# A hybrid decoder layer on one core: tokens loaded in transposed layout, with the RMS-norm row factor applied behind the projections

## The chip, the cores and the metric

The kernel runs on one NeuronCore of a Trainium2 chip. Its time is device time in microseconds, the median of several runs; lower is better.

## What is computed

One decoder layer for 2048 tokens of width 1024, in fp32:

```python
h = rms_norm(x, attn_norm_g)        # x * rsqrt(mean(x*x) + eps) * g
z = h @ w_in                        # q, k, v of attention; q, k, v, gate of retention; pooling input
ya = sliding_window_attention(...)  # 6 query heads, 2 kv heads, window 128, sinks, relative bias
yr = retention(...)                 # 6 heads, chunks of 128, rotary on q and k, recurrent state
yp = pool_mixer(...)                # trailing means over 2, 4, 8, 16 positions
x = x + concat(ya, yr, yp) @ w_out
x = x + square(relu(rms_norm(x, mlp_norm_g) @ w_up)) @ w_down
return rms_norm(x, final_norm_g)
```

The factor rsqrt(mean(x*x) + eps) belongs to a token, the gain g to a channel. In a product h @ w_in the gain has to be in before the sum over channels; the token's factor can be applied to the result.

## The kernel before

The work has two parts. The **mixer** goes through the tokens in four quarters of 512 (`QT`), three in a hardware loop and the last written out with the first steps of the second part mixed in. The **feed-forward part** then goes through all tokens in two passes.

Every large product is made of three matmuls: each operand is split into a high part, rounded to the faster fp32r format on ScalarE (a copy), and a low part, the rest, on VectorE (a subtraction). TensorE sums high x low, low x high and high x high (`three`, lines 2016 to 2018).

A quarter of the mixer runs through 39 output tiles of one PSUM bank each, in three banks in turn (`dense`): tiles 0 to 5 and 22 are projections with channels in partitions (`proj_T`: three of q, then k, v, and twice the pooling input), tiles 6 to 21 are the retention projections with tokens in partitions (`proj_G`), tiles 23 to 38 the output projection (`out_tile`). Between them stand the small products of attention, retention and pooling. Weights come in 27 units of 512 KB a quarter (`NU`), through three staging buffers (`stage`) into a ring of six split pairs: `split_hi` on ScalarE (line 887), `split_lo` on VectorE (line 1550). SyncE (SP) issues the loads in the order of `mixer_loads`; unit u is issued once unit u-3 is split.

The tokens of a quarter are loaded twice. One copy, `xn`, is squared on ScalarE for the row sums (`square_x`, line 906); POOL makes the factor `rstd` (lines 756 and 758); VectorE multiplies by factor and gain (`x_norm`, line 1351); TensorE transposes the result, 8 blocks of 128x128 for each of the four token blocks (`norm_transposes`, line 2045); ScalarE and VectorE split it into `hT_hi` and `hT_lo` (lines 927 and 1358). For the next quarter this is done ahead, between the last output tiles. Tile 0 is made in two halves of 256 tokens (`proj_first`). The other copy, `xq`, is the residual: VectorE adds the output tiles to it (`evac_x2`, line 1507), ScalarE issues its store to DRAM (line 911) and squares it for the second norm (line 919).

At the very start TensorE makes the rows of the relative-position bias (line 2008, fp32, 33 partitions). They go to DRAM and come back shifted.

All engines run fixed orders of instructions and meet at semaphores. A wait holds everything that is behind it on its engine, the DMA issues of SP too.

## Time and profile before

| | us |
|---|---|
| median of 3 runs | 2063.99 |
| lowest, highest | 2061.77, 2064.23 |
| the profiled execution | 2064.74 |
| its span in the trace | 2062.9 |
| TensorE busy | 2036.2 |
| VectorE busy | 1382.3 |
| ScalarE busy | 922.5 |
| POOL busy | 185.9 |

The trace is of one execution. Times in it count from the start of the span. PE is TensorE, DVE VectorE, ACT ScalarE, POOL GpSimd, SP the engine that issues most DMAs. A matmul row shows 0.39 us for 512 columns, but such matmuls overlap; what one costs is the distance between the starts of two.

### The profile page before, as it was taken

The page shows a single profiled execution, that of the slowest core. Times are in us where ns is not written, and L with a number is a line of the kernel's source. Part 1 is how long each engine was busy: PE and PEld are TensorE (multiplying, and loading weights), DVE is VectorE, ACT ScalarE, POOL GpSimd, SP SyncE. Part 2 cuts the span into 40 slices and gives each one's busy share as a digit, 9 for nine tenths or more (in the row PEclk, how much of TensorE's full clock was granted, in tenths as well). Part 3 has the DMA queues.
Part 4 walks back from the last instruction along what each step waited for, and adds up shares of the span by engine and source line. Part 5 has one row for each costly group of instructions (what it writes and reads, how often), then busy time and mean ns, then how long its engine had stood idle before and what let it go on. Part 6 is the DMA issues. An engine that isn't in the chain of part 4 may idle for free.

```text
span 2062.9 us, 28215 instructions
## 1 busy us (share of the span) xinstructions
PE 2036.2 (99%) x10220; PEld 1716.8 (83%) x10220; DVE 1382.3 (67%) x1948; ACT 922.5 (45%) x1557; POOL 185.9 (9%) x259
## 2 busy tenths in 40 slices
PE   8999999999999999999999999999999999999998
PEld 6988898889888987888888888878788888888886
DVE  4576458645764776877777777766766657766666
ACT  4453444445353535545546444445333334433333
POOL 1033003301320321000000000000000000000001
PEclk9999999999999999999999999999999999999999
DMA  6323322342243233577675555677956567846572
GB/s 233 102 93 108 125 95 89 109 151 76 72 159 113 74 125 109 133 172 177 162 168 149 133 153 149 154 213 204 344 223 256 221 263 313 333 189 243 221 285 82
DMA packets 101969, 349.25 MB, mean 169 GB/s; under 512 B 10395, under 2 KB 12220, under 8 KB 84412
## 3 DMA queue, kind: packets, MB, share of 16 engines
q1 hardware_dynamic: 97212, 330.54, 49.8%
q10 hardware_dynamic: 4608, 16.78, 2.1%
q8 instruction: 87, 1.43, 0.3%
q14 instruction: 62, 0.51, 0.1%
HBM read 270.61 MB, written 76.68 MB: 168 GB/s over the span
## 4 chain that ended last, share of the span: by engine, by line
PE 94%; DMA 2%; DVE 1%; ACT 1%; SPq 1%; issue 0%; POOLq 0%; DVEq 0%; ACTq 0%; POOL 0%
PE bank L2016 29%; PE bank L2018 28%; PE bank L2017 28%; PE bank L2125 1%; PE bank L2154 1%; DMA d_raw<-in_wdn 1%; PE bank L2139 1%; PE bank L2202 1%; PE bank L2045 1%; DMA wraw<-in_wup 1%; PE bank L2183 1%; PE bank L2205 1%; PE bank L2245 1%; PE bank L2169 1%; PE bank L2210 1%
## 5 line engine op out<-in xcount | busy, mean ns | idle before, releaser
L2016 PE MATMUL bank<-h_hi,w_lo 128*128 128x512 f32 x912 | 356.7, 391 | 4.4 <-ACT tA L1075 3.1
L2017 PE MATMUL bank<-h_lo,w_hi 128*128 128x512 f32 x912 | 355.6, 390 | 0.0
L2018 PE MATMUL bank<-h_hi,w_hi 128*128 128x512 f32 x912 | 355.4, 390 | 0.0
L2016 PE MATMUL bank<-d_hi,u_lo 128*128 128x512 f32 x896 | 349.0, 390 | 5.0 <-DVE d_lo L1888 5.0
L2018 PE MATMUL bank<-d_hi,u_hi 128*128 128x512 f32 x896 | 348.6, 389 | 0.0
L2017 PE MATMUL bank<-d_lo,u_hi 128*128 128x512 f32 x896 | 348.6, 389 | 0.0
L1225 ACT ACTIVATE u_hi<-u_raw 128x1024 fp32r<-128x1024 f32 x112 | 118.5, 1058 | 334.9 <-PE bank L2018 318.8
L1888 DVE TENSOR_TENSOR u_lo<-u_raw,u_hi 128x1024 fp32r<-128x1024 f32 x112 | 136.9, 1223 | 179.6 <-ACT u_hi L1225 179.6
L2016 PE MATMUL bank<-ring_hi,hT_lo 128*128 128x384 f32 (+1 forms) x672 | 242.7, 361 | 0.0
L2018 PE MATMUL bank<-ring_hi,hT_hi 128*128 128x384 f32 (+1 forms) x672 | 234.4, 349 | 0.0
L2017 PE MATMUL bank<-ring_lo,hT_hi 128*128 128x384 f32 (+1 forms) x672 | 234.1, 348 | 0.0
L2016 PEld LDWEIGHTS bank<-h_hi,w_lo 128*128 128x128 f32 x912 | 171.6, 188 | 41.4 <-DVE w_lo L1733 5.6
L2016 PEld LDWEIGHTS bank<-d_hi,u_lo 128*128 128x128 f32 x896 | 168.2, 188 | 41.4 <-DVE d_lo L1888 6.7
L2018 PEld LDWEIGHTS bank<-h_hi,w_hi 128*128 128x128 f32 x912 | 171.6, 188 | 35.6
L2017 PEld LDWEIGHTS bank<-h_lo,w_hi 128*128 128x128 f32 x912 | 171.7, 188 | 35.2
L2018 PEld LDWEIGHTS bank<-d_hi,u_hi 128*128 128x128 f32 x896 | 168.2, 188 | 35.1
L2017 PEld LDWEIGHTS bank<-d_lo,u_hi 128*128 128x128 f32 x896 | 168.2, 188 | 34.8
L1733 DVE TENSOR_TENSOR w_lo<-wraw,w_hi 128x512 fp32r<-128x512 f32 x156 | 104.1, 686 | 77.4 <-ACT w_hi L1043 76.6
L1550 DVE TENSOR_TENSOR ring_lo<-stage,ring_hi 128x1024 fp32r<-128x1024 f32 x108 | 131.6, 1244 | 28.4 <-ACT ring_hi L887 27.3
L1043 ACT ACTIVATE w_hi<-wraw 128x512 fp32r<-128x512 f32 x156 | 96.6, 626 | 88.5 <-PE bank L2018 88.3
L2016 PEld LDWEIGHTS bank<-ring_hi,hT_lo 128*128 128x128 f32 x672 | 126.2, 188 | 11.0 <-ACT zt L951 2.4
L2018 PEld LDWEIGHTS bank<-ring_hi,hT_hi 128*128 128x128 f32 x672 | 126.2, 188 | 6.6
(198 smaller groups left out, 3161.3 us busy)
## 6 DMA issues: line engine op xcount, KB each, us to landing
u_raw<-u_dram SPq DMA_DIRECT2D x56, 1024.0 KB, 4.8
d_raw<-in_wdn SPq DMA_DIRECT2D x56, 1024.0 KB, 6.9
stage<-in_wmix SPq DMA_DIRECT2D x108, 512.0 KB, 4.2
u_dram<-ur SPq DMA_DIRECT2D x32, 1280.0 KB, 9.4
wraw<-in_wup SPq DMA_DIRECT2D x128, 256.0 KB, 3.4
e_raw<-in_wdn SPq DMA_DIRECT2D x24, 1024.0 KB, 8.9
xn<-in_x SPq DMA_DIRECT2D x16, 512.0 KB, 4.6
xq<-in_x ACTq DMA_DIRECT2D x16, 512.0 KB, 5.7
```

The lines of the kernel that those rows point to most:

```text
L1043: act.activation(w_hi[w_slot(n, k)][:, :, :].rearrange("p c n -> p (c n)"), w_source(n, k), ACT.Copy).then_inc(w_hi_done, 1)
L1225: act.activation(hi[:, cell, :], src[:, 2 * h:2 * h + 2, :], ACT.Copy).then_inc(m_hi_done, 1)
L1550: dve.tensor_tensor(ring_lo[:, s, :], stage[:, u % STAGE, :], ring_hi[:, s, :].bitcast(F32), ALU.subtract).then_inc(wlo_done.sem, 1)
L1733: dve.tensor_tensor(w_lo[s][:, :, :].rearrange("p c n -> p (c n)"), w_source(n, k), w_hi[s][:, :, :].rearrange("p c n -> p (c n)").bitcast ...
L1888: dve.tensor_tensor(lo[:, cell, :], src[:, 2 * h:2 * h + 2, :], hi[:, cell, :].bitcast(F32), ALU.subtract).then_inc(m_lo_done, 1)
L2016: pe.matmul(dst, al, bh, start=(first and k == 0), stop=False, skip_group_check=chain)
L2017: pe.matmul(dst, ah, bl, start=False, stop=False, skip_group_check=chain)
L2018: last = pe.matmul(dst, ah, bh, start=False, stop=(final and k == n - 1), skip_group_check=chain)
L2045: last = pe.transpose(norm_bank(b, j)[:, c * P:(c + 1) * P], xn[:, b, (4 * j + c) * P:(4 * j + c + 1) * P], ident[:, :])
L2125: last = pe.matmul((S0, S1)[g][:, P * h:P * h + P], qT[a:a + HEAD, h, b * P:(b + 1) * P], kT[a:a + HEAD, (b + e) * P:(b + e + 1) * P], sta ...
L2139: last = pe.transpose((T0, T1)[half][:, h * P:(h + 1) * P], score_buf(i // 2)[:, k, 256 * h + P * half:256 * h + P * half + P], ident[:, :])
L2154: last = pe.matmul(OB[a:a + HEAD, 0:384], vtok[:, b + half, a:a + HEAD], pt[:, g, 384 * half:384 * half + 384], start=(half == 0), stop=(h ...
```

## The change

- The host passes the tokens a second time in transposed layout, `xt`. SP loads a quarter of it straight into `xT` in four parts. `xn`, `x_norm`, the transposes and the gain rows are gone. ScalarE makes `hT_hi` with the gain as a scale per partition (`gcol`), VectorE `hT_lo`, channel block by channel block in the order 5, 6, 7, 0 to 4 (`C_ORDER`). For the next quarter, blocks 0 to 4 wait for the last output tile, since they use space that it reads.
- The row factor is applied behind the projections. `square_x` now squares `xq` in the new quarter. POOL makes a diagonal block of factors for each 128 tokens (`diagonal`), and TensorE multiplies it by ones, which gives the factors along the columns in all partitions (`row_factors`, four fp32 matmuls, after tile 2). ScalarE copies them (`rb`). Tiles 3, 5 and 22 are evacuated on VectorE times `rb` (`evac_scaled`), v and the retention tiles on ScalarE with `rstd` as scale, q's factor goes in with the scores.
- Tile 0 is one tile, which waits block by block.
- The four quarters are written out; there is no loop.
- Unit 2 of the first quarter, and units 1 and 2 of the others, are split ahead. The bias rows are made of two fp32r matmuls each instead of one fp32, after 24 warm-up matmuls on ones, and are stored and loaded back between units 4 and 6.
- The x2 store is issued after the square instead of before. The reload of `xq` moves from ScalarE's queue in the middle of a quarter to SP at its end, each block behind the store of the same block.

```diff
 T_GROUP, T_UP1, T_OA, T_OR, NT = 6, 22, 23, 31, 39
+WARM = 24
+C_ORDER = (5, 6, 7, 0, 1, 2, 3, 4)
+X_PARTS = ((5, 6), (6, 8), (0, 2), (2, 5))
...
+
+
+        xT = work("xT", 0, [P, C, QT])
...
+            def load_xt(row, part):
+
+                a, z = X_PARTS[part]
+                sp.dma_start(xT[:, a:z, :].rearrange("p c t -> p (c t)"), xt[row, QT * a:QT * z]).then_inc(x_full[part].sem, 16)
+
+            load_xt(slice(0, P), 0)
+            sp.dma_start(stage[:, 0, :], wmix[0]).then_inc(st_full[0].sem, 16)
+            for part in range(1, len(X_PARTS)):
+                load_xt(slice(0, P), part)
+            for u in range(1, STAGE):
+                sp.dma_start(stage[:, u, :], wmix[u]).then_inc(st_full[u].sem, 16)
             sp.dma_start(ident[:, :], cview("ident")).then_inc(s_ident, 16)
-            sp.dma_start(grow[:, :], gmix.to_broadcast([P, D])).then_inc(s_gain, 16)
-            for b in range(1, NB):
-                sp.dma_start(xn[:, b, :], x[b * P:(b + 1) * P, :]).then_inc(x_full[b].sem, 16)
-            for u in range(STAGE):
...
+            def store_rows():
+                sp.wait_ge(s_brow, NQH)
+                sp.dma_start(rows_dram.rearrange("h (p m) -> p h m", m=384), rrow).then_inc(s_rowst, 16)
+
...
+                    if q == 0 and u == 4:
+                        store_rows()
+                    if q == 0 and u == 5:
+                        load_bias()
                 if last:
                     return
+                row = bass.ds(q * P + P, P)
+                sp.wait_ge(tile_done.sem, tile_done.now(q, T_OR - 1))
+                for part in (0, 2, 3):
+                    load_xt(row, part)
+                load_weights(NU + 1)
+                sp.wait_ge(ro_done.sem, ro_done.now(q, 3))
+                load_xt(row, 1)
+                load_weights(NU + 2)
                 for b in range(NB):
...
+                    sp.wait_ge(x2_stored[b].sem, x2_stored[b].now(q, 0))
+                    sp.dma_start(xq[:, b, :], x[bass.ds(q * QT + (NB + b) * P, P), :]).then_inc(xq_full[b].sem, 16)
+
+            for q in range(NQ - 1):
                 mixer_loads(q, False)
...
+            def diagonal(q, b):
+
+                pool.wait_ge(rstd_done.sem, rstd_done.now(q, b))
+                if b == 0:
+                    pool.wait_ge(qk_done.sem, qk_done.before(q, 3))
+                    pool.wait_ge(rbmm_done.sem, rbmm_done.before(q, 0))
+                pool.tensor_tensor(dg[:, b, :], ident[:, :], rstd[:, b:b + 1].to_broadcast([P, P]), ALU.mult).then_inc(diag_done.sem, 1)
...
+            def square_x(q, b):
+
+                act.wait_ge(xq_full[b].sem, xq_full[b].now(q, 0))
+                if b:
+                    act.wait_ge(sq_done.sem, sq_done.now(q, b - 1))
+                else:
                     act.wait_ge(sq2_done.sem, sq2_done.before(q, NB - 1))
-                    act.wait_ge(sq_done.sem, sq_done.now(q, n - 1))
-                elif n:
-                    act.wait_ge(sq_done.sem, sq_done.now(q, n - 1))
-                act.activation(junk[:, :], xn[:, b, :], ACT.Square, scale=D ** -0.5, accum_out=ssum[:, b:b + 1]).then_inc(sq_done.sem, 1)
-
...
                 act.activation(junk[:, :], xq[:, b, :], ACT.Square, scale=D ** -0.5,
                                accum_out=ssum2[:, bass.ds(q * NB + b, 1)]).then_inc(sq2_done.sem, 1)
-
-            def x_hi(q, b, ahead):
+                act.wait_ge(sq2_done.sem, sq2_done.now(q, b))
+                act.dma_start(x2_dram[bass.ds(q * QT + b * P, P), :], xq[:, b, :]).then_inc(x2_stored[b].sem, 16)
+
+            def x_hi(q, i, ahead):
+
+                c = C_ORDER[i]
+                full = x_full[[a <= c < z for a, z in X_PARTS].index(True)]
+                act.wait_ge(full.sem, full.now(q, 1 if ahead else 0))
                 if ahead:
-                    act.wait_ge(tile_done.sem, tile_done.now(q, T_OA + 9 + 2 * b))
-                for j in range(2):
-                    act.wait_ge(xtr_done.sem, xtr_done.now(q, 2 * NB * ahead + 2 * b + j))
-                    act.activation(hT_hi[:, 4 * j:4 * j + 4, b * P:(b + 1) * P],
-                                   norm_bank(b, j)[:, :].rearrange("p (c t) -> p c t", c=4), ACT.Copy).then_inc(xhi_done.sem, 1)
+                    act.wait_ge(tile_done.sem, tile_done.now(q, NT - 1 if c < 5 else T_UP1))
+                else:
+                    act.wait_ge(s_gain, 16)
+                act.activation(hT_hi[:, c, :], xT[:, c, :], ACT.Copy, scale=gcol[:, c:c + 1]).then_inc(xhi_done.sem, 1)
...
+            def rb_copy(q):
+
+                act.wait_ge(rbmm_done.sem, rbmm_done.now(q, 0))
+                ev, k = evac_of(T_UP1)
+                act.wait_ge(ev.sem, ev.before(q, k))
+                act.activation(rb[:, :], T1[:, :], ACT.Copy).then_inc(rb_done.sem, 1)
...
                 act.wait_ge(tile_done.sem, tile_done.now(q, T_GROUP + t))
                 g, b = t // 4, t % 4
+                act.wait_ge(rstd_done.sem, rstd_done.now(q, b))
                 act.activation(zt[:, b, 384 * g:384 * g + 384], dense[(T_GROUP + t) % 3][:, 0:384],
-                               ACT.Copy).then_inc(z_evac.sem, 1)
+                               ACT.Copy, scale=rstd[:, b:b + 1]).then_inc(z_evac.sem, 1)
...
             def mixer_act(q, last):
-                split_hi(q, 2)
+                evac_T(q, 0)
+                square_x(q, 0)
+                square_x(q, 1)
                 split_hi(q, 3)
+                evac_T(q, 1)
+                square_x(q, 2)
+                square_x(q, 3)
                 split_hi(q, 4)
+                evac_T(q, 2)
                 split_hi(q, 5)
-                for t in range(5):
-                    evac_T(q, t)
-                    split_hi(q, t + 6)
-                evac_T(q, 5)
+                split_hi(q, 6)
+                rb_copy(q)
+                split_hi(q, 7)
+                split_hi(q, 8)
+                evac_T(q, 4)
+                split_hi(q, 9)
+                split_hi(q, 10)
...
+                    square_x2(q, 1)
+                    for i in range(3):
+                        x_hi(q, i, True)
+                    square_x2(q, 2)
+                    for i in range(3, C):
+                        x_hi(q, i, True)
                     split_hi(q, NU + 1)
-                    square_x2(q, 3, last)
-
-            for b in range(NB):
-                square_x(0, b)
+                    square_x2(q, 3)
+                    split_hi(q, NU + 2)
...
+            x_hi(0, 0, False)
             split_hi(0, 0)
-            for b in range(NB):
-                x_hi(0, b, False)
+            for i in range(1, C):
+                x_hi(0, i, False)
             split_hi(0, 1)
-            with act.Fori(0, NQ - 1) as q:
+            split_hi(0, 2)
+            for q in range(NQ - 1):
...
+            def x_lo(q, i, ahead):
+
+                c = C_ORDER[i]
+                dve.wait_ge(xhi_done.sem, xhi_done.now(q, C * ahead + i))
+                dve.scalar_tensor_tensor(out=hT_lo[:, c, :], in0=xT[:, c, :], scalar=gcol[:, c:c + 1],
+                                         in1=hT_hi[:, c, :].bitcast(F32), op0=ALU.mult, op1=ALU.subtract).then_inc(xlo_done.sem, 1)
+
+            def evac_scaled(q, t):
+
+                dve.wait_ge(tile_done.sem, tile_done.now(q, t))
+                dve.wait_ge(rb_done.sem, rb_done.now(q, 0))
+                if t == 3:
+                    dve.wait_ge(carried.sem, carried.now(q, 0))
+                    dst = kT[:, P:P + QT]
+                else:
+                    dve.wait_ge(carried.sem, carried.now(q, 2))
+                    dst = up[:, 0 if t == 5 else 1, PADW:PADW + QT]
+                dve.scalar_tensor_tensor(out=dst, in0=dense[t % 3][:, :], scalar=SCALE if t == 3 else 1.0, in1=rb[:, :],
+                                         op0=ALU.mult, op1=ALU.mult).then_inc(s_evac.sem, 1)
 
...
-                                             in0=(S0, S1)[g][:, 0:384].rearrange("p (h m) -> p h m", h=3), scalar=SCALE,
+                                             in0=(S0, S1)[g][:, 0:384].rearrange("p (h m) -> p h m", h=3), scalar=rstd[:, b:b + 1],
...
-                    norm_ahead(q, 3, last)
                     evac_x2(q, 12)
-                    x_lo(q, 1, True)
+                    for i in range(3):
+                        x_lo(q, i, True)
                     evac_x2(q, 13)
-                    x_lo(q, 2, True)
                     evac_x2(q, 14)
                     evac_x2(q, 15)
-                    x_lo(q, 3, True)
+                    for i in range(3, C):
+                        x_lo(q, i, True)
                     split_lo(q, NU + 1)
-
...
-            pe.wait_ge(s_relw, 1)
+            pe.wait_ge(s_init, 2)
+            for _ in range(WARM):
+                pe.matmul(bank[0][:, 0:P], ones[:, :], ones[:, :], start=True, stop=True)
+            pe.wait_ge(s_relw, 3)
             for h in range(NQH):
-                pe.matmul(bank[h][:, 0:384], relw[:, h, :], oneh, start=True, stop=True).then_inc(s_browmm, 1)
-            pe.wait_ge(s_ident, 48)
-            pe.wait_ge(s_brow, NQH)
+                pe.matmul(bank[2 + h][:, 0:384], relw_lo[:, h, :], oneh_r, start=True, stop=False)
+                pe.matmul(bank[2 + h][:, 0:384], relw_hi[:, h, :], oneh_r, start=False, stop=True).then_inc(s_browmm, 1)
...
+            def row_factors(q):
...
+                pe.wait_ge(diag_done.sem, diag_done.now(q, NB - 1))
+                for b in range(NB):
+                    last = pe.matmul(T1[:, b * P:(b + 1) * P], ones[:, :], dg[:, b, :], start=True, stop=True)
+                last.then_inc(rbmm_done.sem, 1)
+
+            def proj_T(q, t):
+
+                pe.wait_ge(wlo_done.sem, wlo_done.now(q, t if t < 6 else 18))
+                free_bank(q, t)
...
+                for i, c in enumerate(C_ORDER):
+                    if t == 0:
+                        pe.wait_ge(xlo_done.sem, xlo_done.now(q, i))
+                    last = three(dense[t % 3][:, :], [(wh[:, c, :], wl[:, c, :], hT_hi[:, c, :], hT_lo[:, c, :])],
+                                 first=(i == 0), final=(i == C - 1))
+                last.then_inc(tile_done.sem, 1)
...
             def mixer_pe(q, closing):
-                proj_first(q, 0)
-                proj_first(q, 1)
-                for t in range(1, 5):
+                for t in range(4):
                     proj_T(q, t)
+                    if t == 2:
+                        row_factors(q)
+                proj_T(q, 4)
                 att_scores(q, 0)
```

The order on **SP at a join** of two quarters. Before (stage: weight units; xn: tokens to be normalised):

```order
L567 DMA xn<-in_x 128x1024
L552 REGISTER_ALU
L553 DMA stage<-in_wmix 128x1024
L552 REGISTER_ALU
L553 DMA stage<-in_wmix 128x1024
L566 REGISTER_ALU
L567 ISA
L567 DMA xn<-in_x 128x1024
L569 REGISTER_ALU
L569 COMPARE_AND_BRANCH
L548 DMA tabs<-in_tab 128x544
L553 DMA stage<-in_wmix 128x1024 x24
```

Now (xT: transposed tokens; xq: the residual tokens; tabs: tables):

```order
L583 DMA stage<-in_wmix 128x1024 x22
L543 DMA xT<-in_xt 128x512
L543 DMA xT<-in_xt 128x1024
L543 DMA xT<-in_xt 128x1536
L583 DMA stage<-in_wmix 128x1024
L543 DMA xT<-in_xt 128x1024
L583 DMA stage<-in_wmix 128x1024
L603 DMA xq<-in_x 128x1024 x4
L578 DMA tabs<-in_tab 128x544
L583 DMA stage<-in_wmix 128x1024 x25
```

The four residual loads stand ahead of the tables and of units 3 and later of the next quarter; before, no token load with a wait for a store was on SP.

The order on **ScalarE at the same place**. Before:

```order
L927 ACTIVATE hT_hi<-bank 128x4x128
L884 REGISTER_ALU
L887 ACTIVATE ring_hi<-stage 128x1024
L910 REGISTER_ALU
L911 DMA x_dram<-xq 128x1024
L919 ISA
L919 ACTIVATE junk,ssum_55<-xq 128x1024
L1203 REGISTER_ALU
L1203 COMPARE_AND_BRANCH
L887 ACTIVATE ring_hi<-stage 128x1024 x4
L945 ACTIVATE qT<-bank 128x512
L887 ACTIVATE ring_hi<-stage 128x1024
```

Now:

```order
L961 ACTIVATE hT_hi<-xT,small 128x512 x5
L929 ACTIVATE ring_hi<-stage 128x1024
L947 ACTIVATE junk,ssum_55<-xq 128x1024
L950 DMA x_dram<-xq 128x1024
L929 ACTIVATE ring_hi<-stage 128x1024
L978 ACTIVATE qT<-bank 128x512
L938 ACTIVATE junk,ssum<-xq 128x1024 x2
L929 ACTIVATE ring_hi<-stage 128x1024
L978 ACTIVATE qT<-bank 128x512
L938 ACTIVATE junk,ssum<-xq 128x1024 x2
L929 ACTIVATE ring_hi<-stage 128x1024
L978 ACTIVATE qT<-bank 128x512
```

The five high parts stand ahead of the last square and store of the old quarter, and the two pairs of squares (junk,ssum<-xq) now stand in the new quarter, one on each side of the evacuation of tile 1.

**TensorE before tile 3.** Before, at the end of a quarter (xn: normalised tokens):

```order
L2032 REGISTER_ALU
L2035 REGISTER_ALU
L2045 MATMUL bank<-ident,xn 128x128 x4
L2035 REGISTER_ALU
L2045 MATMUL bank<-ident,xn 128x128 x4
L2026 REGISTER_ALU
L2016 MATMUL bank<-ring_hi,hT_lo 128x512
L2017 MATMUL bank<-ring_lo,hT_hi 128x512
```

Now, in the first quarter:

```order
L2073 MATMUL bank<-hT_lo,ring_hi 128x512
L2074 MATMUL bank<-hT_hi,ring_hi 128x512
L2093 MATMUL bank<-dg,ones 128x128 x4
L2072 MATMUL bank<-hT_hi,ring_lo 128x512
L2073 MATMUL bank<-hT_lo,ring_hi 128x512
```

The transposes are gone, and the product of the diagonal blocks stands between the last matmul of tile 2 and the first of tile 3.

## Rows read from the trace of the kernel before

**Rows 1.** The page, part 1: busy time of each engine.
```profile
PE 2036.2 (99%) x10220; PEld 1716.8 (83%) x10220; DVE 1382.3 (67%) x1948; ACT 922.5 (45%) x1557; POOL 185.9 (9%) x259
```

**Rows 2.** The waits of TensorE, whole run: total us, times, longest.
```profile
PE bank L2008 <- DVE zt L1346: 5.6, 1, 5.6
...
PE bank L2016 <- DVE d_lo L1888: 5.0, 4, 2.0
...
PE bank L2045 <- DVE hT_lo L1358: 2.3, 1, 2.3
```

**Rows 3.** Busy us by engine, window 60 to 560 us.
```profile
60.00:560.00 500.00, 499.71 (x3025) 438.61 (x3024) 311.43 (x541) 222.08 (x476) 111.84 (x132) 1.00 0.30 103
```

**Rows 4.** Timeline of TensorE, start: start us, us, instruction, [idle before <-releaser].
```profile
5.60 8.01 PE L2008 MATMUL bank<-zt 33*128 33x384 f32 x12 [5.60 <-DVE zt L1346]
...
20.27 3.62 PE L2045 MATMUL bank<-ident,xn 128*128 128x128 f32 x16 [2.31 <-DVE hT_lo L1358]
...
23.57 0.43 PE L2016 MATMUL bank<-hT_hi,ring_lo 128*128 128x256 f32 x1
...
45.81 0.39 PE L2016 MATMUL bank<-hT_hi,ring_lo 128*128 128x512 f32 x1
```

**Rows 5.** The chain that ended last, before the first join.
```profile
192.63 0.67 PE bank L2210 x6
...
213.47 0.87 PE bank L2045 x8
```

**Rows 6.** Timeline of TensorE at the first join.
```profile
214.65 0.39 PE L2018 MATMUL bank<-ring_hi,hT_hi 128*128 128x512 f32 x1
...
217.37 0.39 PE L2018 MATMUL bank<-ring_hi,hT_hi 128*128 128x512 f32 x1
...
223.76 0.40 PE L2016 MATMUL bank<-hT_hi,ring_lo 128*128 128x512 f32 x1
```

**Rows 7.** Windows in the start, last column GB/s moved.
```profile
2.00:8.00 6.00, 2.40 (x4) 1.50 (x5) 0.70 (x1) 2.43 (x3) 3.79 (x7) 1.00 0.80 228
...
8.00:16.00 8.00, 7.30 (x17) 4.05 (x16) 6.14 (x9) 5.07 (x8) 2.42 (x6) 1.00 1.02 412
```

**Rows 8.** Timeline of ScalarE and POOL, row sums in the start.
```profile
11.25 1.06 ACT L906 ACTIVATE junk<-xn 128x1024 bf16<-128x1024 f32 x1
...
12.53 1.06 ACT L906 ACTIVATE junk<-xn 128x1024 bf16<-128x1024 f32 x1
...
13.76 0.19 POOL L756 TENSOR_TENSOR var<-ssum,epsc 128x1 f32<-128x1 f32 x1 [0.24 <-ACT junk L906]
...
14.03 0.54 POOL L758 TENSOR_TENSOR rstd<-var,mhalf 128x1 f32<-128x1 f32 x1
```

**Rows 9.** One line on POOL, 128x384, all quarters: ns min/median/max.
```profile
L795 POOL TENSOR_TENSOR R<-R,gch x16: 996/1046/1202, 158.1 to 775.1; 128x384 f32<-128x384 f32 x16
```

**Rows 10.** VectorE and ScalarE: join, eight of h_hi, one line with a scale vector.
```profile
217.80 0.69 DVE L1507 TENSOR_TENSOR xq<-bank,xq 128x512 f32<-128x512 f32 x1 [3.51 <-PE bank L2018]
...
813.27 4.27 ACT L1057 ACTIVATE h_hi<-hraw 128x512 fp32r<-128x512 f32 x8
...
L1018 ACT ACTIVATE hT_hi<-bank,pscale x8: 687/688/688, 159.6 to 750.5; 128x512 fp32r<-128x512 f32 x8
```

**Rows 11.** Landing times: x2 stores (line 911), and one weight unit at 200 us.
```profile
DMA to landing us min/median/max: 2.6/2.8/5.1
...
stage<-in_wmix SPq DMA_DIRECT2D x1, 512.0 KB, 3.4
```

**Rows 12.** TensorE after a wait of 2.48 us; the window of 5 us after.
```profile
1353.46 0.47 PE L2016 MATMUL bank<-h_hi,w_lo 128*128 128x512 f32 x1 [2.48 <-ACT tA L1075]
...
1355.30 0.63 PE L2017 MATMUL bank<-h_lo,w_hi 128*128 128x512 f32 x1
...
1355.73 0.63 PE L2018 MATMUL bank<-h_hi,w_hi 128*128 128x512 f32 x1
...
1355.00:1360.00 5.00, 5.00 (x17) 3.95 (x16) 3.18 (x5) 1.66 (x4) 0.00 (x0) 0.67 0.37 117
```

More of the change, by code:

```diff
@@ L827, in mixer_pool @@
             def mixer_pool(q, last):
+                for b in range(NB):
+                    inv_rms(q, b)
+                    diagonal(q, b)
                 rot_b(q, 0)
@@ L843, in mixer_pool @@
                 ret_scale(q, 2)
-                if not last:
-                    for n in range(3):
-                        inv_rms(q, NB + n)
                 decay_state(q, 3)
@@ L1163, in mixer_act @@
                 evac_qkT(q, 3)
[L1164 to L1166 removed]
                 yR_high(q, 2)
                 ret_out(q, 3)
[L1169 removed]
+                square_x2(q, 0)
                 if last:
```

327 lines of the change are left out of this document (131 added, 196 removed).

## The prediction

> **What bounds the kernel now.** I read the page first, then the list of waits, then windows by stage. TensorE is busy for 2036.2 of 2062.9 us [rows 1], so only two things can change the time: how much TensorE has to do, and where it waits. Its listed waits come to some 19 us: among them one of 5.6 us before the bias-row matmuls, four with 5.0 us together in the down projection, and one of 2.3 us in the first transposes [rows 2]. From 60 to 560 us, nearly three of the four quarters, it is busy 499.71 of 500 us [rows 3]. So in the mixer nothing is waited for, and every microsecond of TensorE work that goes is a microsecond won, provided no new wait appears.
>
> The start is the exception. The first projection matmul comes at 23.57 us, tile 3 of the first quarter ends at 45.81 us [rows 4]. Before that TensorE works at the lower of its two clocks: 16 transposes take 3.62 us [rows 4], 0.226 us each, and later 8 take 0.87 us [rows 5], 0.109 us each. That is 1.2 against 2.4 GHz, although it had been busy with the bias rows (12 passes of 384 columns in 8.01 us, with 33 of 128 rows in use) for most of the time since 5.60 us.
>
> **The start, up to the end of tile 3.** Gone are the 32 transposes, the wait for the normalised tokens, and the row sums ahead of the first product. Two paths lead to the new end of tile 3, and the later one decides.
>
> *TensorE's path.* The 24 warm-up matmuls are fp32, two passes of 128 columns each, so 48 passes. A fast pass costs 0.11 us (six of L2210 in 0.67 us [rows 5]), a slow one 0.22. Starting at about 2.1 us, I let 5 us run slow (22 passes) and the rest fast (26 x 0.11 = 2.9 us): done at 10.0. The bias rows are now 12 single passes of 384 columns at 0.17 us (three quarters of the step between 512-column matmuls, which is 0.227 us: 12 steps from 214.65 to 217.37 us [rows 6]), done at 12.0. Tile 0 is 24 x 0.227 = 5.44 us, end 17.4; its tokens and its weight split are there by 15 us, since all that it needs is the first 2.6 MB of the loads (11 us by the rates below) and the splits of the last three blocks. Tiles 1 and 2 end at 28.3.
>
> *The data path.* The row factors stand on TensorE between tiles 2 and 3. They need all four row sums of squares; ScalarE makes the last two only after it has split weight unit 3. Up to and with unit 3 the queue carries 2.10 MB of transposed tokens, 1.57 MB of three units, 2.10 MB of tokens, 1.06 MB of constants and 0.52 MB: 7.35 MB. The trace moved 228 GB/s in the 6 us from 2 to 8 us and 412 GB/s after that [rows 7]: 1.37 MB by 8 us, the other 5.98 MB in 14.5 us, so 22.5, and with 0.7 us of my own allowance for the landing, 23.2. From there: split 1.05, evacuation 0.55, two squares at 1.28 each (one starts at 11.25 us, the next at 12.53 [rows 8]), variance and power on POOL 0.8 [rows 8], the diagonal block 0.45, two hand-overs of 0.1: 5.6 us. The diagonal operation isn't in the trace; it lies between 0.19 us for one column on POOL [rows 8] and 1.05 for 384 [rows 9], and I take 0.45. Row factors start at 28.8, half a microsecond after TensorE is there. They are 4 fp32 matmuls, 8 passes, 0.9 us; tile 3 ends at 29.7 + 5.44 = 35.1 instead of 45.81: **-10.7 us**.
>
> The 412 GB/s row speaks against a figure of the Trainium skill: its page "DMA: Bandwidth & Descriptors", section "Specifications", gives about 358 GB/s per core from HBM. By that figure the 5.98 MB would take 16.7 us, and the gain at the start would be about 2 us smaller. The measurement decides.
>
> **The three joins between quarters.** T is the moment when TensorE has issued the last output matmul of a quarter (217.37 + 0.23 = 217.60 us at the first join [rows 6]).
> - Transposes: four groups of 8 at 0.87 us go: -3.5 us.
> - Tile 0 in two halves and the loop's back edge take from 217.60 to 223.76, 6.16 us [rows 6]; as one tile 5.44: -0.7 us.
> - Row factors: +0.9 us.
> - Tile 0 now has to wait for tokens written into space that the last output tile reads. TensorE starts with channel blocks 5 to 7, which are free early: 9 matmuls, 2.0 us. In that time VectorE finishes its last x2 sum (217.80 + 0.69, so T+0.9 [rows 10]) and the low part of block 0 (0.65 us). Each later block costs VectorE and ScalarE less than TensorE's 0.68 us, so this is hidden; the split of unit 1 is late by some 0.1 us: +0.1 us. If VectorE were a microsecond later, all of that would show.
> - The row factors are late. ScalarE does five high parts of tokens (0.53 us each by the eight of h_hi in 4.27 us, 0.69 with a scale vector from PSUM [rows 10]; I take 0.63), to T+3.45; splits unit 1, T+4.5; squares the last x2 block, T+5.75; only then issues the store, which lands 2.8 us later (the median, between 2.6 and 5.1 [rows 11]), T+8.55. SP waits for that store before it reloads the last token block, and the tables and weight unit 3 are queued behind it on SP. A lone 512 KB load lands in 3.4 us [rows 11]; 0.80 MB of tables and unit add 1.95: unit 3 lands at T+14.0. ScalarE has its split in front of the last two squares, so the same 5.6 us follow: T+19.6. TensorE is there at T + 3 x 5.44 + 0.1 = T+16.4. **+3.2 us**, between 0 (all earlier than I think) and 7.
>
> Per join -3.5 - 0.7 + 0.9 + 0.1 + 3.2 = 0.0: what the transposes give back, the wait takes.
>
> **The clock after such a wait.** At 1353.46 us TensorE had stood for 2.48 us; soon after, its matmuls were 0.43 us apart (1355.30 and 1355.73) instead of 0.227, and the granted clock was 0.67 over that 5 us window [rows 12], which is a stretch at 1.2 GHz. Eight slow matmuls cost 8 x 0.2 = 1.6 us. The four waits of up to 2.0 us in the down projection [rows 2] show no such fall. A wait of 3.2 us is beyond the one that was punished; I count two of three joins: **+3.2 us** (between 0 and 4.8).
>
> Rest: VectorE takes over three evacuations a quarter from ScalarE (0.7 us each) and loses four normalisations of 1.28 us; TensorE's order leaves both engines microseconds of room there, so nothing. The last x2 stores are 1.3 us later; the first token reads of the feed-forward part are of quarters 0 and 1, long stored: nothing. If VectorE's room in the score stage were gone, a tile would come about 1 us late in each quarter.
>
> **Sum**: -10.7 + 0.0 + 3.2 = -7.5 us. The profiled execution took 2064.74 us (span 2062.9), 0.75 above the median of the runs shown; 2064.74 - 7.5 - 0.75 gives **2056.5 us**. 0.2% of the time, about what a measurement tells from no change, is 4.1 us: the borders are 2059.9 and 2068.1.
>
> **Rivals.**
> *The joins are free* (0.23). The store lands early or POOL's part is short, and the wait is under 1.5 us, too short for the clock to fall. At no wait at all: 3 x 3.2 and 3.2 us less, 2043.7; at 1.5 us, 2048. For it: the store can land in 2.6 us [rows 11]. Against it: the chain has nine links in series, each from a row.
> *The start gives less* (0.22). The warm-up isn't enough, or the 33-row bias matmuls behind it let the clock stay low. Then 48 passes take 10.6 us, the bias rows 4, tile 0 at the lower clock nearly 8: tile 0 ends near 24 instead of 17.4, and the time is about 2062.6. For it: 8 us of bias rows left the clock low in the trace. Against: the warm-up uses all 128 rows.
> *Slower* (0.06). At the joins SP stands at the last store, and units 3, 4 and 5 queue behind. If the DMA engines there give 228 GB/s as in the first microseconds and the store takes 5 us [rows 11], unit 3 lands at T+18.5 and each join waits 7.7 us, with the slow clock each time: 3 x 4.5 + 1.6 = 15 us more, 2071.6. It decides from a landing at about T+17.
> *It does not do what it says* (0.07): with the tokens transposed the start is bound by loads all the same, because 2 MB of plain tokens are loaded beside them before unit 3; tile 3 ends near 40 us, 2061.
>
> **How the numbers follow.** The forecast has 0.42 and its own range is 2052 to 2060. The range 2046 to 2063 adds most of the free joins and of the weaker start, and leaves out the slower case and joins without any wait. Faster by over 0.2% holds the forecast but for its upper edge, the free joins and a little of the weaker start: 0.67. Within 0.2%: 0.25. Slower: 0.08.
>
> **What would show it.** Tile 3 of the first quarter ends near 35 us. At each join, between tile 2 and the row factors, TensorE waits about 3 us for POOL's diagonal, which follows the last square, which follows the split of unit 3. After at least one of them matmuls are 0.43 us apart. In the list of waits the new line is the largest. Wrong would be: no such line (then the time is below 2050), a projection that begins after 20 us, or a wait at the first matmul of tile 0 in later quarters.

## The result, and the profile after

The changed kernel takes **2069.85 us** (median of 8 runs, 2064.34 to 2073.66), the kernel before, measured with it, 2062.64 (8 runs, 2061.77 to 2064.95). The ratio is 1.0031, with an interval of 1.0022 to 1.0041: slower, by 7 us where 7.5 less had been forecast, and outside the range of 2046 to 2063. The profiled execution took 2069.51 us. The page has for it:

```profile
span 2067.1 us, 27056 instructions
...
PE 2031.5 (98%) x10076; PEld 1709.9 (83%) x10076; DVE 1381.7 (67%) x1946; ACT 928.0 (45%) x1561; POOL 188.9 (9%) x278
```

TensorE has 144 instructions fewer than in [rows 1], but only 4.7 us less busy time, since some of it now runs at the lower clock. It stands still for longer. Its waits, total us, times, longest:

```profile
PE bank L2093 <- POOL dg L804: 17.3, 4, 5.5
PE bank L2072 <- DVE d_lo L1943: 4.5, 4, 2.4
PE bank L2062 <- POOL ones L779: 2.6, 1, 2.6
```

The first line is new, and it is the wait that the prediction named: TensorE, before the row-factor matmuls, for POOL's diagonal. It comes in the first quarter and at each of the three joins. The timeline of TensorE has the first of them, and the second, at the first join:

```profile
28.72 0.39 PE L2074 MATMUL bank<-hT_hi,ring_hi 128*128 128x512 f32 x1
33.13 1.13 PE L2093 MATMUL bank<-dg,ones 128*128 128x128 f32 x8 [4.03 <-POOL dg L804]
...
41.15 0.39 PE L2072 MATMUL bank<-hT_hi,ring_lo 128*128 128x512 f32 x1
...
209.27 0.39 PE L2072 MATMUL bank<-hT_hi,ring_lo 128*128 128x512 f32 x1
...
225.80 0.39 PE L2074 MATMUL bank<-hT_hi,ring_hi 128*128 128x512 f32 x1
230.26 2.05 PE L2093 MATMUL bank<-dg,ones 128*128 128x128 f32 x8 [4.07 <-POOL dg L804]
231.96 0.77 PE L2072 MATMUL bank<-hT_hi,ring_lo 128*128 128x512 f32 x1
...
235.09 0.63 PE L2073 MATMUL bank<-hT_lo,ring_hi 128*128 128x512 f32 x1
235.52 0.45 PE L2074 MATMUL bank<-hT_hi,ring_hi 128*128 128x512 f32 x1
```

41.15 is the first matmul behind tile 3 of the first quarter (it was 45.81 in [rows 4]), and 209.27 the T of the first join (217.60 before). From 231.96 to 235.52 eight matmuls are 0.445 us apart on average, much as in [rows 12]: the lower clock. The windows around the four waits show the same in the column behind POOL, the granted clock:

```profile
33.00:38.00 5.00, 4.87 (x19) 4.04 (x20) 1.23 (x1) 0.52 (x2) 0.00 (x0) 0.66 0.97 282
...
225.00:240.00 15.00, 10.93 (x42) 8.88 (x41) 5.32 (x5) 8.59 (x12) 3.31 (x6) 0.77 0.50 167
240.00:380.00 140.00, 140.00 (x875) 123.22 (x874) 93.73 (x167) 60.48 (x137) 30.39 (x32) 1.00 0.25 83
...
425.00:440.00 15.00, 10.28 (x42) 8.79 (x42) 6.03 (x7) 8.05 (x11) 3.31 (x6) 0.77 0.43 140
...
625.00:635.00 10.00, 8.26 (x33) 6.83 (x34) 3.58 (x4) 5.16 (x7) 1.51 (x2) 0.83 0.53 180
```

Between the joins TensorE is full (140.00 of 140 us). So the lead of the changed kernel can be followed from join to join. T, the start of the first instruction behind a quarter's last output matmul, for the third quarter and the fourth:

```profile
606.07 0.39 PE L2072 MATMUL bank<-hT_hi,ring_lo 128*128 128x512 f32 x1
...
807.87 0.92 PE L2289 MATMUL bank<-ident,hx 128*128 128x128 f32 x7
```

| | before | after | lead |
|---|---|---|---|
| tile 3 of quarter 0 ends | 45.81 | 41.15 | 4.66 |
| T of join 1 | 217.60 | 209.27 | 8.33 |
| T of join 2 | 411.89 | 407.33 | 4.56 |
| T of join 3 | 606.14 | 606.07 | 0.07 |
| last quarter ends | 801.31 | 807.87 | -6.56 |
| span | 2062.9 | 2067.1 | -4.2 |

A lead of 8.33 us at the first join (4.66 of the start, and 3.7 of the quarter, where the transposes are no longer made) is eaten up behind the three joins, 3.8, 4.5 and 6.6 us. The feed-forward part, whose instructions the change hardly touches, takes 2.4 us less in this execution. The one before had the wait of 2.48 us of [rows 12] and the lower clock behind it; the one after doesn't have that wait, but the lower clock behind one of 2.40 us at 1480.71 us.

Why is the diagonal late? The timelines of ScalarE, SP, POOL and VectorE at the first join (T = 209.27):

```profile
212.61 1.05 ACT L929 ACTIVATE ring_hi<-stage 128x1024 fp32r<-128x1024 f32 x1
213.56 1.04 ACT L947 ACTIVATE junk<-xq 128x1024 bf16<-128x1024 f32 x1
...
214.72 0.33 ACTq L950 DMA_DIRECT2D x_dram<-xq  x1
...
223.83 1.06 ACT L929 ACTIVATE ring_hi<-stage 128x1024 fp32r<-128x1024 f32 x1 [4.83 <-DMA stage<-in_wmix]
...
226.50 1.06 ACT L938 ACTIVATE junk<-xq 128x1024 bf16<-128x1024 f32 x1
```
```profile
218.24 0.33 SPq L603 DMA_DIRECT2D xq<-in_x  x1
218.66 0.38 SPq L578 DMA_DIRECT2D tabs<-in_tab  x1
219.08 7.42 SPq L583 DMA_DIRECT2D stage<-in_wmix  x4
```
```profile
227.37 0.40 POOL L804 TENSOR_TENSOR dg<-ident,rstd 128x128 f32<-128x128 f32 x1
...
228.63 1.49 POOL L804 TENSOR_TENSOR dg<-ident,rstd 128x128 f32<-128x128 f32 x1
```
```profile
228.63 1.23 DVE L1604 TENSOR_TENSOR ring_lo<-stage,ring_hi 128x1024 fp32r<-128x1024 f32 x1 [2.48 <-ACT ring_hi L929]
```

This is the predicted chain, link by link: x_hi, split of unit 1, square, store at T+5.45, reload of the token block at T+9.0, tables, unit 3, ScalarE idle for 4.83 us until unit 3 is there (T+14.56), its split ahead of the last two squares, POOL, TensorE at T+20.99. New is the last diagonal: 1.49 us instead of 0.40, and VectorE's subtraction for unit 4 begins in the same hundredth of a microsecond.

### The profile page after: what moved, and what is told of

Read it like the earlier page. It is cut to its first block, busy times and chain, and to the rows that moved or that the text cites. A ratio compares the mean times of both kernels' runs of the same rounds, so it can differ in the third digit from the quotient of the medians.

```text
span 2067.1 us, 27056 instructions
## 1 busy us (share of the span) xinstructions
PE 2031.5 (98%) x10076; PEld 1709.9 (83%) x10076; DVE 1381.7 (67%) x1946; ACT 928.0 (45%) x1561; POOL 188.9 (9%) x278
## 4 chain that ended last, share of the span: by engine, by line
PE 91%; DMA 3%; DVE 2%; ACT 1%; SPq 1%; issue 1%; POOL 1%; POOLq 0%; ACTq 0%; DVEq 0%
PE bank L2072 28%; PE bank L2074 27%; PE bank L2073 27%; PE bank L2169 1%; PE bank L2198 1%; DMA d_raw<-in_wdn 1%; PE bank L2183 1%; PE bank L2246 1%; DMA stage<-in_wmix 1%; PE bank L2227 1%; PE bank L2249 1%; PE bank L2289 1%; DMA wraw<-in_wup 1%; PE bank L2213 1%; PE bank L2254 1%
## 5 line engine op out<-in xcount | busy, mean ns | idle before, releaser
L929 ACT ACTIVATE ring_hi<-stage 128x1024 fp32r<-128x1024 f32 x108 | 109.7, 1056 | 66.5 <-DMA stage<-in_wmix 40.4
```

The costliest lines, as they stand in the source:

```text
L929: act.activation(ring_hi[:, SLOT[u % NU], :], stage[:, u % STAGE, :], ACT.Copy).then_inc(whi_done.sem, 1)
```

## The experiments

**Theory W**: the change saves what it was priced at, and loses by the four waits for the diagonal (17.3 us) and the lower clock behind them. By the step of the matmuls (in the first quarter 8 at 0.427 instead of 0.227 us, 1.6 us; at the first two joins the row factors too, 0.8 us each) the clock costs 1.6, 2.5, 1.8 and 1.6 us: 25 us in all. Rivals: the longer program of the written-out quarters, the warm-up, the bytes and the order of the loads. The kernels e1 to e12 are the changed kernel with one edit each where nothing else is said; e8 is the kernel before.

**1. Row factors behind tile 3** (TensorE has 5.4 us more work before it needs the diagonal; VectorE's scaled evacuation of tile 3 follows later).
```
-                    if t == 2:
+                    if t == 3:
                         row_factors(q)
```


> The row factors move on TensorE from behind tile 2 to behind tile 3; nothing else changes. Theory W (the changed kernel loses its gain in the four waits for the diagonal blocks, 17.3 us, and in the slow clock after them, some 9 us): the diagonal is ready 4 to 5.5 us after the end of tile 2 and a tile takes 5.4, so all four waits go and the clock does not fall; about 2045 us. Rival V (the weights are what is late: units 3 and later are queued behind the residual reload, and the wait only moves): tile 3 then waits for the split of unit 3; in the trace of the changed kernel that split ended 0.0, 1.4 and 0.1 us after tile 2 at the joins, later tiles would wait too, and the time stays above 2060 us.


Measured: 2045.04 us (2043.57 to 2047.05), ratio to before 0.9913 (0.9897 to 0.993), as forecast.

**2. Squares 2 and 3 ahead of the split of unit 3** (in ScalarE's program; the token blocks that they need land before unit 3 does, at the first join the last of them some 2 us before it).
```
                 square_x(q, 1)
-                split_hi(q, 3)
                 evac_T(q, 1)
                 square_x(q, 2)
                 square_x(q, 3)
+                split_hi(q, 3)
                 split_hi(q, 4)
```


> ScalarE makes the last two squares of a quarter before it splits unit 3, the row factors stay behind tile 2. Theory W with the chain as predicted (unit 3's landing is the link that makes the squares late): the squares start when tile 1 and the residual block are there, T+12.5, the row factors are ready at about T+16 against T+16.9 on TensorE, the waits fall from 4.4 us to under 1 us each, in the first quarter to under 0.5; but unit 3's split ends no earlier, so tile 3 waits up to 1.5 us. About 2047 us. If something else in the chain were late (POOL, the store), the waits would stay above 3 us and the time at 2065 or more.


Measured: 2043.47 us (2041.77 to 2044.69), ratio 0.9903 (0.9887 to 0.992), 3.5 us less than expected. In both the line of the diagonal is gone from TensorE's waits; of the first run they begin:
```profile
PE bank L2072 <- DVE d_lo L1943: 4.3, 4, 2.4
PE bank L2062 <- POOL ones L779: 2.6, 1, 2.6
PE bank L2072 <- DVE ring_lo L1604: 2.3, 3, 1.3
```
So either edit takes away the whole loss, 24.8 and 26.4 us, as theory W has it (25). What the two edits have in common is that wait.

**3. Both.**


> Row-factor matmuls behind the fourth tile, and the two squares ahead of the split of unit 3. Theory W (the change loses by the four waits for the diagonals and the slower clock behind them): either edit alone already leaves no wait for a diagonal (2045.04 and 2043.47 us), so both together bring nothing more: 2042 to 2046 us, granted clock 0.999 or more. Rival (the two edits take away different costs, each some 25 us): near 2020 us.


Measured: 2046.88 us (2042.93 to 2047.65). That is 0.9 us above the expected range, and nothing more is gained. The cost was one and the same.

**4. Fill the wait**: 14 fp32 matmuls of 128 columns on ones (28 passes) ahead of the row factors. They compute nothing that is used.
```
+                for _ in range(14):
+                    pe.matmul(T1[:, 0:P], ones[:, :], ones[:, :], start=True, stop=True)
                 pe.wait_ge(diag_done.sem, diag_done.now(q, NB - 1))
```


> Fourteen matmuls of ones stand on TensorE ahead of the wait for the diagonal, 28 passes, 3.1 us at the full clock; they fill the wait and compute nothing that is used. If the lower clock after the waits costs what its rows say (2.1 to 2.6 us a join, 1.6 in the first quarter), the clock stays up, the diagonal comes when it came, and the time falls by some 8 us, to about 2061. If the clock's share were small, or the filling delayed the row factors, the time would stay at 2069 or rise.


Measured: 2053.64 us (ratio 0.9955, 0.9939 to 0.9972), with a mean granted clock of 0.999 (0.993 in the changed kernel). Filling each wait with 3 us of useless matmuls is 16 us faster than waiting in quiet. I expected 2061. In this run's profiled execution the last diagonal took 0.40 us each time, not 1.49, and the fill covered all of the wait: at the first join the row factors come 3.1 us behind the last matmul of tile 2, and no clock falls. That led to the question of runs 5 and 6.

**5. No warm-up.**
```
-WARM = 24
+WARM = 0
```


> No warm-up matmuls. The changed kernel waits 4 us before the first row factors, whose time is set by ScalarE and the loads, so by theory W a slower start on TensorE of up to 4 us is hidden by that wait: tile 0 starts at about the same time, runs part of it at the lower clock, ends some 3 us later, and the total stays within 1 us of 2069. If the warm-up itself were worth its price, the time would rise by 3 us or more.


Measured: 2056.1 us (2053.42 to 2059.79), 13.7 us faster than the changed kernel, where I had expected no more than 1 us: the surprise of this study. At the start its bias rows run 0.32 us apart instead of 0.17, and the lead of the warm-up at the first T is 0.5 us (209.75 against 209.27). The gain comes after that. One line of POOL in the changed kernel, and in this one (ns min/median/max):
```profile
L804 POOL TENSOR_TENSOR dg<-ident,rstd x16: 400/402/1488, 21.9 to 625.1; 128x128 f32<-128x128 f32 x16
```
```profile
L804 POOL TENSOR_TENSOR dg<-ident,rstd x16: 398/400/403, 21.9 to 617.2; 128x128 f32<-128x128 f32 x16
```
At the first join the last diagonal starts at 228.33 us here, and VectorE 10 ns behind it; now VectorE's instruction is the one that lasts longer, 1.47 instead of 1.23 us:
```profile
228.34 1.47 DVE L1604 TENSOR_TENSOR ring_lo<-stage,ring_hi 128x1024 fp32r<-128x1024 f32 x1 [2.48 <-ACT ring_hi L929]
```
In the changed kernel POOL lost the tie in all four places, here in none: 4 x 1.09 us. The remaining 2.7 us of the 7.1 that TensorE waits less come from unit 3, split at T+13.7 to 13.8 in place of T+14.2 to 16.0. Why the ties and unit 3 come out otherwise without a warm-up no run shows. The mixer also loses 1.8 us less to the clock: behind the waits of 2.21 and 2.24 us it fell, behind the one of 2.18 us at the second join it did not (first window below; the second shows the third join). The feed-forward part of this execution is 2.9 us shorter, with a wait of 1.34 us and no slow clock where the changed kernel had 2.40 us and a slow clock. 7.1 + 1.8 + 2.9 is the 11.8 us between the two spans.
```profile
418.00:428.00 10.00, 7.82 (x39) 6.34 (x38) 5.02 (x4) 7.54 (x11) 2.22 (x6) 1.00 0.60 220
...
612.00:622.00 10.00, 7.76 (x32) 6.23 (x31) 5.01 (x4) 7.54 (x11) 2.22 (x6) 0.83 0.61 223
```

**6. Break the tie**: ScalarE evacuates tile 2 before it splits unit 4, which puts VectorE 0.5 us behind POOL.
```
-                split_hi(q, 4)
                 evac_T(q, 2)
+                split_hi(q, 4)
```


> ScalarE clears the bank of tile 2 before it splits unit 4, so that VectorE's low half of unit 4 starts some 0.6 us behind the last diagonal instead of with it. Theory D (the last diagonal lasts 1.49 us in the changed kernel because a VectorE subtraction of 1.23 us that began in the same 10 ns went first): the last diagonal lasts 0.40 us in each quarter, each of the four waits is 1.1 us shorter, 4.4 us in all, with up to 3 us of slow clock less besides: 2061 to 2066 us against 2069.85. Rival (the 1.49 us come from something else on GpSimd): still 1.49, and 2069 to 2071 us.


Measured: 2062.44 us (2058.15 to 2068.25), 7.4 us less than the changed kernel, ratio to before 1.0 (0.999 to 1.001). All 16 diagonals last 400 to 403 ns, and the waits sum to 13.5 us instead of 17.3. So the 1.49 us are the tie. "SBUF — State Buffer" of the Trainium skill, section "Who interferes with whom", says that a VectorE instruction with two inputs in SBUF contends with a GpSimd instruction that reads SBUF, and that the order of issue decides who blocks. The rows agree that one of the two is held up: VectorE's delay is 0.24 us and GpSimd's 1.09, less than the other's whole instruction (0.40 and 1.23). They don't show the order of issue. In the 35 places of these runs where the last diagonal and the subtraction start together, GpSimd's record is the first to start; where VectorE's follows by 1 to 5 ns (eight places) GpSimd is the one held up, where it follows by 5 to 17 ns (27 places) VectorE is.

**7. Store before the square.** The last x2 block is stored when it is complete; the reload waits for the square as well.
```
                 act.wait_ge(x2_evac.sem, x2_evac.now(q, 8 + 2 * b + 1))
+                act.dma_start(x2_dram[...], xq[:, b, :]).then_inc(x2_stored[b].sem, 16)
...
-                act.wait_ge(sq2_done.sem, sq2_done.now(q, b))
-                act.dma_start(x2_dram[...], xq[:, b, :]).then_inc(x2_stored[b].sem, 16)
...
                     sp.wait_ge(x2_stored[b].sem, x2_stored[b].now(q, 0))
+                    sp.wait_ge(sq2_done.sem, sq2_done.now(q, b))
```


> Each row block is stored before ScalarE squares it instead of after (the reload of that block then waits for the square as well). Theory S (the waits of the joins hang on the chain last evacuation, square, store, reload of the row block, load of unit 3, split, squares, diagonal): the last store goes out 1.2 us sooner, unit 3 is split 1.0 to 1.2 us sooner after each of the three joins, the waits there are each about 1.1 us shorter, and the last diagonal may or may not fall together with VectorE's subtraction: 2062 to 2067 us, 2066 if the diagonals keep their 1.49 us. Rival (unit 3 is late because of what is queued ahead of it in bytes, not because of the store): unit 3 is split at the same distance from the join, within 0.3 us, and 2069 to 2071 us.


Measured: 2046.8 us (2045.36 to 2048.06), ratio 0.9921 (0.9904 to 0.9937): 23 us less where I expected 3 to 8. ScalarE and SP at the first join, whose T is 209.76 in this kernel:
```profile
210.02 1.34 ACT L961 ACTIVATE hT_hi<-xT,small 128x512 fp32r<-128x512 f32 x2 [4.61 <-PE bank L2074]
210.68 0.33 ACTq L944 DMA_DIRECT2D x_dram<-xq  x1
...
221.38 1.06 ACT L930 ACTIVATE ring_hi<-stage 128x1024 fp32r<-128x1024 f32 x1 [2.48 <-DMA stage<-in_wmix]
```
```profile
215.26 0.33 SPq L604 DMA_DIRECT2D xq<-in_x  x1
215.68 0.98 SPq L578 DMA_DIRECT2D tabs<-in_tab  x1
216.71 1.37 SPq L583 DMA_DIRECT2D stage<-in_wmix  x3
```
The store stands in the program behind five x_hi and a split, yet it goes out at 210.68 us, when three x_hi and the split have not begun. ScalarE's queue had passed them all on and stopped only at what the store itself waits for, the sum that ends at 210.65. In the changed kernel the same queue stopped at the wait for the square's own result. So the store went out at T+0.9 instead of T+5.45, 4.5 us earlier and not 1.2; the reload now waits for the square, and goes 3.5 us earlier; unit 3 is split at T+11.6 instead of T+14.56. At the joins TensorE waits no more than 0.1 us: the only line of the diagonal left is the 4.5 us of the start. Theory S holds as to the chain; its size was too small, since it didn't count on the queue running ahead.

**8. The kernel before with its loop written out.**
```
-            with pe.Fori(0, NQ - 1) as q:
+            for q in range(NQ - 1):
                 mixer_pe(q, False)
...
```
(and so on all five engines)


> The kernel before, with its loop over three quarters written out and nothing else. Theory W prices the written-out quarters at nothing: 2061.5 to 2063.5 us. Rival (a larger program is slow to fetch, and that is what the changed kernel lost by): 2066 to 2072 us. Rival (the jump back costs the kernel before something at each join): 2058 to 2061 us.


Measured: 2062.59 us (2060.29 to 2064.59), ratio 0.9998 (0.9989 to 1.0008). The written-out quarters cost nothing and bring nothing.

**9. Constants behind unit 5.** The nine loads of constants leave the head of SP's queue, and VectorE's wait for them moves behind the split of unit 8.
```
-            sp.dma_start(cmask[:, :], cview("mask")).then_inc(s_const, 16)
...
                     if q == 0 and u == 5:
+                        load_consts()
                         load_bias()
...
                 split_lo(q, 8)
+                if q == 0:
+                    dve.wait_ge(s_const, 16 * 9)
```


> The changed kernel with its nine loads of constants (7.4 us of issue on SP's queue, 9.4 to 16.6 us) moved behind the load of unit 5; VectorE waits for them ahead of the first scores. Theory Q (at the start unit 3 is late because SP issues it at 18.4 us, behind the constants and the table): it is issued by 13 us and is split by 23.5 us instead of 26.7, the first wait for a diagonal falls from 4.03 us to 1.1 or less, and the time by 3 to 5.5 us: 2064 to 2067 us against 2069.85. Rival (the bytes of the row blocks ahead of it hold it back, at the 408 GB/s of that stretch): split at 25.5 us or later, and 2068 to 2071 us.


In the changed kernel, and in this one, SP has at the start:
```profile
9.36 0.45 SPq L554 DMA_DIRECT2D cmask<-in_cst  x1
...
13.21 3.40 SPq L562 DMA_DIRECT2D poolw<-in_pool_w  x4
16.73 1.66 SPq L578 DMA_DIRECT2D tabs<-in_tab  x1
18.43 1.29 SPq L583 DMA_DIRECT2D stage<-in_wmix  x2
```
```profile
9.59 0.36 SPq L579 DMA_DIRECT2D tabs<-in_tab  x1
10.00 7.79 SPq L584 DMA_DIRECT2D stage<-in_wmix  x2
```
Issued 8.4 us earlier, at 10.0 instead of 18.43 us, unit 3 is split only 2.1 us earlier, at 24.64 instead of 26.70: between the two forecasts, and theory Q doesn't explain it. In the changed kernel the DMA engines had no gap that an earlier issue could have filled. The windows (last three columns: clock, DMA busy share, GB/s) and unit 3's time from issue to landing:
```profile
18.00:20.00 2.00, 2.00 (x11) 1.65 (x10) 2.00 (x6) 1.64 (x4) 0.00 (x0) 1.00 1.03 407
20.00:22.00 2.00, 2.00 (x11) 1.65 (x10) 1.18 (x2) 1.14 (x2) 1.77 (x3) 1.00 1.10 295
22.00:24.00 2.00, 2.00 (x11) 1.65 (x10) 0.00 (x0) 0.00 (x0) 1.44 (x4) 1.00 1.03 339
24.00:26.00 2.00, 2.00 (x11) 1.65 (x9) 0.28 (x2) 0.00 (x0) 0.00 (x0) 1.00 1.02 399
...
DMA to landing us min/median/max: 8.2/8.2/8.2
```
The table, issued just before unit 3, landed at 25.72 us. What run 9 took out of the way is the 0.67 MB of the constants, an estimate of 1.6 us at 408 GB/s, and the slow stretch from 20 to 24 us, in which the small loads move:
```profile
20.00:24.00 4.00, 4.00 (x20) 3.30 (x18) 1.93 (x5) 0.63 (x2) 2.63 (x5) 1.00 1.01 394
```
By these rows unit 3 was late by what the DMA engines had to move, not by when SP issued it. The first wait fell from 4.03 to 1.29 us (1.1 of it the tie, won here at the start), with no slow clock behind it. The time, 2058.88 us (2054.3 to 2065.41), fell by 11 us, more than the start can give; the profiled execution, with a span of 2063.6 us, accounts for 3.5. The other 7 are not seen in it. It lost its tie at all three joins, and executions that win some would be faster; that is an argument, not a measurement. The shorter executions did have more clock: 0.998 of full speed at 2054.3 us, 0.993 at 2065.41.

**10. All three reorders** (squares first, stores first, constants behind unit 5).


> Squares ahead of the split of unit 3, stores ahead of the squares, constants behind unit 5, all in one. Theory W (only TensorE's waits and the slower clock behind them are lost, and they are gone with the first edit alone, 2043.47 us): 2041 to 2045 us, no wait for a diagonal, PE idle in all within 1 us of the second run's. Rival (each edit also brings what it brought alone): below 2035 us.


Measured: 2041.81 us (2040.44 to 2042.91), ratio 0.9901 (0.9884 to 0.9917). That is inside theory W's range, and no wait for a diagonal is left: the three edits together bring 1.7 us more than the squares alone.

**11. Run 3 without the warm-up, 12. run 10 without the warm-up.**


> The third kernel of the study (row factors behind the fourth tile, squares first) without the 48 warm-up passes. Theory W (the warm-up moves the first quarter's end by some 0.5 us, and what the run without it gained came from diagonals of 0.40 instead of 1.49 us and shorter waits at the joins, which this kernel does not have): 2046 to 2049 us, within 2 us of 2046.88. Rival (the warm-up itself costs what that run gained, 13.7 us): near 2033 us.

> The kernel with all the reordered steps (squares first, stores first, constants behind unit 5; 2041.81 us) without the 48 warm-up passes. Theory W (where no join waits, the warm-up moves the first quarter's end by half a microsecond and nothing else): 2040.5 to 2043 us. Rival (the warm-up itself costs some 3 us, as between the two runs with row factors behind the fourth tile, 2046.88 and 2043.57 us): 2038 to 2039.5 us.


Measured: 2043.57 us (2042.74 to 2044.62) against 2046.88, and 2041.35 (2040.28 to 2041.88) against 2041.81. The first pair differs by 3.3 us, more than the 2 that I allowed; the second, with narrower spreads, does not differ, although the warm-up had its first T 1.4 us earlier (203.06 against 204.48). The 13.7 us of run 5 are in neither, so they were not the price of the warm-up itself but of the waits. Run 12 is the best version: 0.9898 (0.9882 to 0.9915) of the kernel before, 21 us faster, without 48 of the instructions of the change.

## Why the prediction was wrong

The mechanisms were those forecast: the chain at the join, its place, its releaser, and the clock behind it. What failed was the size of the waits, by three terms of the sum: the landing of unit 3, the last diagonal block, and the clock. In the terms of the sum, against the two profiled executions (+4.8 us, where -7.5 was forecast, 12.3 us off):

- **The start, -10.7 forecast, -4.7 measured.** The row factors begin at 33.13 us, not 28.8. Unit 3 was put at 23.2 us; it landed at 26.68 and was split at 26.70. That is the largest single step that failed, 3.5 us. The sum stopped at the 7.35 MB up to and with unit 3, at 412 GB/s. By the packets in the trace 8.5 MB had been moved when unit 3 landed, 1.1 MB of them of unit 4 and of the store of the bias rows, both issued behind it: about 2.7 us at 412 GB/s. And from 8 to 26.7 us the rate was 383 GB/s, which is 1.3 us more; the 0.7 us allowed for the landing was not needed. SP's late issue at 18.43 us was not the cause (run 9). The last diagonal took 1.49 us where 0.45 stood, 1.0 us. And the wait of 4.03 us brings the slow clock, 1.6 us, where the half microsecond of the forecast was priced without. The warm-up (end at 10.3 us, forecast 10.0), the bias rows at 0.17 us and tiles 1 and 2 (end 28.95, forecast 28.3) came as worked out. The rival of the weaker start named another cause, a clock that stays low; it did rise.
- **The joins: row factors at T+19.6 forecast, at T+20.99, 22.38 and 20.66 measured**, 5.2 us more in all; TensorE's own arrival is 0.4 us later than forecast, and its waits are 4.07, 5.46 and 3.78 us instead of 3.2. Unit 3 was split at T+14.56, 15.96 and 14.24 (forecast 14.0), 2.8 us in all, and from there to the row factors it took 6.4 us instead of 5.6, for the lost tie. 0.45 for the diagonal was right for 12 of 16; a bound by the nearest row of POOL never asked what VectorE does at that moment.
- **The clock, +3.2 forecast, 5.9 at the joins measured**: 2.7 us more. All three waits were punished, not two, with 8, 5 and 8 slow matmuls, and at the first two joins the row factors themselves were slow (2.05 us instead of 1.13).
- **The remaining terms** (transposes -3.5, tile 0 -0.7, row factors +0.9) fit the quarters. With the late row factors and the clock they give losses of 3.9 and 4.6 us behind the first two joins, where the table shows 3.8 and 4.5; behind the third, with no transposes saved, 6.1 where it shows 6.6. The feed-forward part gave 2.4 us back that the change doesn't account for.

6.0 + 5.2 + 2.7 - 2.4 is 11.5 of the 12.3 us; 0.6 us more lie outside the spans, which differ by 4.2 us where the times differ by 4.8. The joins priced at 0.0 were a balance of large terms, -4.2 + 4.2 a join, in which a chain of nine links in series decided. Each link beyond forecast went fully into the time, and the clock came on top. The slower rival was given 0.06 with a landing of T+17 as its border; it needed only T+14 to 16 and a slow diagonal. The rival of free joins, which runs 1, 2 and 7 made real, was put at 2043.7 us; these runs took 2045.0, 2043.5 and, with the start's wait still there, 2046.8.

What stays open is the spread of unit 3: in the kernels that store behind the square, unit 3 is split anywhere from T+13.6 to T+16.6. No run shows what sets that, nor what sets the few nanoseconds of the tie.

## What to carry to other kernels

When a change puts a late value in front of the engine that bounds the kernel, look for the link in its chain that has no need to be there: here three different edits of a few lines each (consumer later, producers ahead of a wait for data, store ahead of the square) were each worth over 20 us, and the combinations (runs 3 and 10) brought at most 1.7 us more than the best of them alone. Price a long wait on TensorE with the clock on top: here 17.3 us of waits cost 7.5 us of clock. Price a landing by all that the DMA engines move before it, small loads and what is issued behind it included. And where two engines are released by the same instruction, ask what each does to the other.

## What the runs showed of the hardware

- A GpSimd multiply of 128x128 took 0.40 us by itself. When a VectorE subtraction of two SBUF tiles began within 17 ns of it, one of the two was held up: GpSimd took 1.49 instead of 0.40 us, or VectorE 1.47 instead of 1.23. A few nanoseconds decided over 1.09 us on the critical path.
- TensorE's granted clock fell to 1.2 GHz behind waits of 2.21, 2.24, 2.40, 3.78, 4.03, 4.07 and 5.46 us, and stayed at 2.4 GHz behind 1.29, 2.18 and one of 2.39 us (run 1). So the length of a wait between 2.2 and 2.4 us doesn't tell by itself whether the clock falls. The wait of run 1, with matmuls 0.23 us apart behind it (1459.54, 1459.77, 1460.00):
```profile
1459.20 0.50 PE L2072 MATMUL bank<-d_hi,u_lo 128*128 128x512 f32 x1 [2.39 <-DVE d_lo L1943]
```
- A DMA issued by ScalarE went out ahead of four of its own earlier instructions that had not yet begun (run 7, at 210.68 us): it stood behind its waits, not behind the work written before it.
- With the DMA engines busy throughout, a stretch with many small loads moved 295 and 339 GB/s, the stretches around it 407 and 399.
- Fourteen useless matmuls ahead of each wait made the kernel 16 us faster (run 4); an estimate of 4.4 us of that is the tie, won in its profiled execution.
